# The first norm's sum of squares: sixteen ones products on TensorE behind the projection's blocks, in place of sixteen VectorE additions

## What is computed

```python
def rmsnorm(x, g):
    xf = x.astype(F32)
    y = xf * lax.rsqrt(jnp.mean(xf * xf, axis=-1, keepdims=True) + RMS_EPS)
    return (y * g.astype(F32)).astype(x.dtype)

def s5_layer(h, g_pre, ...):
    xn = rmsnorm(h, g_pre)
    uz = xn @ w_in                 # 2048 x 4096
    u, z = jnp.split(uz, 2, axis=-1)
    y = s5_ssm(u, ...)             # needs powers of the state's poles, made from its parameters
    ...
```

## Time and profile before

| | |
|---|---|
| median of 3 runs | 3483.96 us |
| the three runs | 3482.14, 3483.96, 3485.89 us |
| profiled execution, device time | 3486.52 us |
| its span in the profile | 3484.7 us |
| PE busy | 3246.0 us (93%) |
| PEld busy | 2529.4 us (73%) |
| DVE busy | 1435.7 us (41%) |
| ACT busy | 1145.8 us (33%) |
| POOL busy | 1619.3 us (46%) |

### The profile page before, as it was taken

How to read it: one execution, slowest core, us unless ns; L and a number is a source line. 1 busy time by engine, 2 the same in 40 slices (tenths; PEclk the granted TensorE clock), 3 DMA queues, 4 the chain that set the end, 5 groups by cost and what they waited for, 6 DMA issues and landing times.

```text
span 3484.7 us, 48561 instructions
## 1 busy us (share of the span) xinstructions
PE 3246.0 (93%) x18540; PEld 2529.4 (73%) x18540; DVE 1435.7 (41%) x2229; ACT 1145.8 (33%) x1500; POOL 1619.3 (46%) x1292
## 2 busy tenths in 40 slices
PE   5799998999899999999989889999999999967797
PEld 4688886878668787878868757777777777734486
DVE  8777783120242222222230144444534534546512
ACT  4344442233333332322342333323223323315521
POOL 2566662444557667777744424344444434400142
PEclk9899998999999999999999999999999999978899
DMA  3555555232212222222212222222212212211222
GB/s 129 156 155 161 160 164 156 96 143 88 95 57 80 81 84 84 84 84 84 82 61 99 84 103 82 82 74 85 81 71 73 89 68 83 79 57 48 92 92 94
DMA packets 117903, 332.97 MB, mean 96 GB/s; under 512 B 58512, under 2 KB 61712, under 8 KB 86544
## 3 DMA queue, kind: packets, MB, share of 16 engines
q1 hardware_dynamic: 117776, 331.08, 28.2%
HBM read 296.96 MB, written 29.36 MB: 94 GB/s over the span
## 4 chain that ended last, share of the span: by engine, by line
PE 73%; issue 16%; POOL 5%; DVE 4%; ACT 1%; DMA 0%; ACTq 0%; SPq 0%; POOLq 0%; DVEq 0%
PE bank L159 21%; PE bank L161 20%; PE bank L160 20%; POOL wlo L146 4%; PE bank L1308 2%; PE bank L1014 1%; PE bank L1032 1%; PE bank L422 1%; ACT whi L140 1%; PE bank L421 1%; PE bank L433 1%; PE bank L407 1%; PE bank L1023 0%; PE bank L999 0%; PE bank L1288 0%
## 5 line engine op out<-in xcount | busy, mean ns | idle before, releaser
L146 POOL TENSOR_TENSOR wlo<-wraw,whi 128x512 fp32r<-128x512 f32 x912 | 1245.3, 1397 | 1685.9 <-ACT whi L140 1685.8
L159 PE MATMUL bank<-rhi,whi 128*128 128x512 f32 x3648 | 1494.2, 410 | 108.3 <-POOL wlo L146 37.5
L160 PE MATMUL bank<-rlo,whi 128*128 128x512 f32 x3648 | 1433.8, 393 | 0.0
L161 PE MATMUL bank<-rhi,wlo 128*128 128x512 f32 x3648 | 1433.7, 393 | 0.0
L159 PEld LDWEIGHTS bank<-rhi,whi 128*128 128x128 f32 x3648 | 691.8, 190 | 326.2 <-issue 92.7
L161 PEld LDWEIGHTS bank<-rhi,wlo 128*128 128x128 f32 x3648 | 691.8, 190 | 148.9
L160 PEld LDWEIGHTS bank<-rlo,whi 128*128 128x128 f32 x3648 | 693.3, 190 | 140.9 <-issue 11.3
L140 ACT ACTIVATE whi<-wraw 128x2048 fp32r<-128x2048 f32 x228 | 437.0, 1917 | 617.9 <-PE bank L161 471.0
L845 POOL TENSOR_TENSOR wraw<-wraw,vec 128x512 f32<-128x512 f32 x260 | 266.3, 1056 | 0.0
L753 DVE TENSOR_TENSOR ssum<-ssum,wk 128x512 f32<-128x512 f32 x30 | 21.6, 719 | 311.4 <-ACT wk L743 311.4
L743 ACT ACTIVATE wk<-bank 128x512 f32<-128x512 f32 x32 | 27.8, 870 | 236.7 <-PE bank L161 236.7
(11 more groups left out here) (351 smaller groups left out, 3252.5 us busy)
## 6 DMA issues: line engine op xcount, KB each, us to landing
wraw<-in_wall_dram SPq DMA_DIRECT2D x228, 1024.0 KB, 4.8
g<-in_bmat_dram SPq DMA_DIRECT2D x16, 512.0 KB, 5.4
g<-scr_e SPq DMA_DIRECT2D x128, 64.0 KB, 4.8
scr_a<-ssum SPq DMA_DIRECT2D x32, 256.0 KB, 2.1
g<-in_xp_dram SPq DMA_DIRECT2D x4, 1024.0 KB, 11.7
g<-in_cmat_dram SPq DMA_DIRECT2D x16, 256.0 KB, 4.5
scr_u<-wk SPq DMA_DIRECT2D x16, 256.0 KB, 5.9
scr_y<-wk SPq DMA_DIRECT2D x16, 256.0 KB, 2.2
```

The source lines that it names most:

```text
L146: ins = pool.tensor_tensor(wlo[:, slot, c], wraw[:, slot, c], whi[:, slot, c].bitcast(F32), ALU.subtract)
L159: pe.matmul(acc[slot][:, :], whk, rhi[:, k, :], start=(k == 0), stop=False)
L160: pe.matmul(acc[slot][:, :], whk, rlo[:, k, :], start=False, stop=False)
L161: ins = pe.matmul(acc[slot][:, :], wlk, rhi[:, k, :], start=False, stop=(k == KT - 1))
```

## The change

The square of each block is no longer added by DVE. PE multiplies it by the ones matrix right behind the block's three products, accumulating over the 16 blocks in the norm's PSUM bank, and PE's ones product increments `ssq`, which gives ACT its square buffer back. The final ones product over `ssum` goes. The square root waits for `ssq` at 16 in place of `st_mm`; the later waits on `st_mm` count one less.

```diff
-        def split_lo(d, src, gain, base, square=None, ks=range(KT)):
+        def split_lo(d, src, gain, base, ks=range(KT)):
...
-                if square is not None:
-                    add_square(d, *square, k)
-
-        def add_square(d, sqb, sbase, k):
-
-            d.wait_ge(sq_f, sbase + k + 1)
-            wait(d, ssq, sbase + k)
-            if isinstance(k, int) and k == 0:
-                d.tensor_copy(ssum[:, :], sqb[0]).then_inc(ssq, 1)
-            else:
-                d.tensor_tensor(ssum[:, :], ssum[:, :], sqb[k % 2], ALU.add).then_inc(ssq, 1)
...
-        def project_summing(pe, n, slot, r_base, sq_base):
+        def project_summing(pe, n, slot, r_base, sq_base, sqb):
...
-            norm_root(act, V_EPS6, st_mm, 1)
+            norm_root(act, V_EPS6, ssq, 16)
...
-            split_lo(d, g1, V_G1, 0, (sqb0, 0))
+            split_lo(d, g1, V_G1, 0)
...
-            project(pe, 0, 0, wait_r=0)
-            norm_sum(pe, 0)
+            project_summing(pe, 0, 0, 0, 0, sqb0)
...
-            project_summing(pe, N_GATE, 0, 48, 16)
+            project_summing(pe, N_GATE, 0, 48, 16, sqb)
```

More of the change, by code:

```diff
@@ L1856, in _ @@
                 act_out(act, n, n % 2, n // 2, n - 48, V_GPOST0, 16, True, scaled=(n - 62) or None)
-            norm_root(act, V_EPS6, st_mm, 2)
+            norm_root(act, V_EPS6, st_mm, 1)
             act.wait_ge(gemm, N_GATE)
@@ L1877, in _ @@
             act_out(act, N_LORA - 1, 0, (N_LORA - 1) // 2, 15, V_GPOST1, 48, False)
-            norm_root(act, V_EPS6, st_mm, 3)
+            norm_root(act, V_EPS6, st_mm, 2)
             act.wait_ge(gemm, N_LORA)
@@ L1911, in _ @@
             act_last(act, 227, 1, 113, 15, more=False)
-            norm_root(act, V_EPS5, st_mm, 4)
+            norm_root(act, V_EPS5, st_mm, 3)
         @block.vector
@@ L2016, in _ @@
             norm_sum(pe, 3)
-            project_summing(pe, N_LORA, 1, 80, 32)
+            project_summing(pe, N_LORA, 1, 80, 32, sqb)
             for n in range(N_LORA + 1, N_RWKV + 4):
```

## The result

| | median | runs |
|---|---|---|
| before | 3485.81 us | 20 (3481.14 to 3494.22) |
| changed | 3493.11 us | 20 (3487.58 to 3500.11) |
| ratio | 1.0017 | 95% interval 1.0010 to 1.0024 |

By the ratio the change costs 5.9 us (3.5 to 8.4), by the medians 7.3 us. A second set, 12 runs of the changed kernel beside 29 of before, gave a ratio of 1.0019 (1.0009 to 1.0029). The kernel is slower: both intervals leave out 1. The profiled execution took 3492.37 us (span 3490.6), the one of before 3486.52 (span 3484.7). On the page of the profile DVE's busy time fell from 1435.7 to 1428.4 us and PE's rose from 3246.0 to 3256.5.

The account below looks back on a forecast made before the run. DVE bounded the first norm's stage at 1.27 us a block; PE at 1.56 takes over. Block 15's square, root and reciprocal come 7.8 us later, undiminished to the end: 3483.96 + 7.8 = 3491.8 us, 8-in-10 range 3486 to 3495.5.

Parts of the forecast that it names:

- What bounds: First norm's stage: DVE sets the rhythm at 1.27 us a block, ACT is next at 1.13 us.
- PE's block: First norm's stage, changed: three products 0.69 us plus ones product 0.87 us, so 1.56 us a block at full rate.
- The ring of square buffers: ACT's square of block k waits for ones product k-2; 1 us of room, so PE runs unstalled.
- The ramp: PE's start at 26.19 us: half rate for 5.0 us, each microsecond of it costing 0.48 us.
- The tail on ACT: End of the norm: square of block 15 at 50.67 us, `whi`, table load, root at 54.4, 0.6 us after PE.
- No drain beside the table load: ACT's table load before the root: no drain in the rows; the page's 1.38 us would make the sum 9.2 us.
- Rigid path: From reciprocal past the handover at 153.57 us to the end: the 7.8 us delay passes through undiminished.
- a sign against it: Whole kernel: the forecast would be wrong if the end moved by another amount than the handover.
- The number: Whole kernel: 7.8 us slower, median 3491.8 us, 0.22% more; 63 in 100 for slower by over 7.0 us.
- The cheap ones product: Rival, norm stage: ones product under 0.43 us, ACT sets the rhythm, 3482 us, no measurable change; 4 in 100.
- Half rate throughout: Rival, norm stage: PE stays at half rate, 2.99 us a block, some 28 us more, 3512 us; 4 in 100.
- Absorption: Rival, DVE's part behind the norm: hidden slack leaves 0 to 4 us, 3484 to 3488 us; 9 in 100.

Follow-up runs that it names:

- e_both: Kernel before, DVE's additions kept, with an unused ones product on x behind each block of tile 0; one run 3490.92 us beside 3487.42.
- e_warm: Changed kernel with seven unused ones products on PE ahead of block 0; 3491.30 us beside 3487.42, ratio 1.0009.
- e_root_first: Changed kernel with ACT's root ahead of `whi` of tile 1; one run 3492.80 us.
- e_f32r_early: Changed kernel with one-pass ones products, three square buffers, early parameter operations and first power step ahead of the reciprocal; 3480.52 us beside 3485.74, ratio 0.9980.
- e_double: Changed kernel with each of the first norm's sixteen ones products done twice; 3508.06 us beside 3487.42 for before, ratio 1.0054.
- e_early: Changed kernel with DVE's first 15 parameter operations moved between the blocks' rests and ACT's sines moved earlier; 3486.62 us beside 3485.74, ratio 0.9999.
- e_f32r: Changed kernel with squares and ones in the 32-bit type PE takes in one pass; 3485.48 us beside 3487.42, ratio 0.9996.
- e_before_early: Kernel before, DVE's additions kept, with 15 parameter operations moved early between the blocks' rests; 3486.50 us beside 3486.65, ratio 1.0001.
- e_f32r_early2: Changed kernel with one-pass ones products, three square buffers and early parameter operations, first power step left behind `z_scale`; 3477.38 us beside 3486.65, ratio 0.9971.
- changed again: The changed kernel itself, unaltered, measured once more against before; 3492.81 us beside 3485.74, ratio 1.0019.

## Why the prediction was right

**What bounds.** DVE held the stage at 1.27 us a block and PE had too little room; the additions' removal is in the timeline as 0.81 us of idle DVE time. Right.

**PE's block.** 1.56 us forecast, 1.55 us measured, and two records in every block, unstalled. The price came from the two places where line 786 stood already. This term carried the forecast; doubling it doubled the delay and a one-pass product removed it.

**The ring of square buffers.** ACT waits in it 0.30 us a block, but PE never waits for a square: right, and `e_both`, with ones products and without that wait, shows the same delay.

**The ramp.** 5.0 us assumed, 4.3 us in the profiled execution: the record at 29.88 in the changed kernel (0.55 us) is the first shortened one. Starting at full rate gave 1.97 us back, which is 0.46 us for each of the 4.3, beside 0.48 in the sum.

**The tail on ACT.** Root directly behind the table load: right. The square of block 15 came at 49.96 us instead of 50.67 and the reciprocal at 54.43 instead of 55.1. Of these 0.7 us PE's earlier start explains 0.3 and the shorter ramp another 0.3. Counted from PE's start the reciprocal is 7.3 us later; the sum said 7.8.

**No drain beside the table load.** In the changed kernel the root follows the start of its load by 53.71 - 52.41 = 1.30 us, and this time nothing else could have hidden a drain: PE's last ones product had ended at 53.03. Ahead of the next load there is none either: the root ends at 54.40 and the load starts at 54.41. The estimate of 9.2 us from the Trainium skill ("ScalarE: Activation LUTs", "What ACT_TABLE_LOAD costs") is refuted for this place; the measurement decides.

**Rigid path.** 7.04 us at the reciprocal, 7.49 at the handover, 5.85 at the last reciprocal. No delay was absorbed up to the handover: right. The 0.45 us that it grew come just ahead of the handover, most of them where DVE's line 352 idles 0.69 us for PE's line 433 instead of 0.26. So DVE does wait for PE there, which the prediction's "and not the other way" passed over. Behind the handover the end moved by another amount than the handover did, and the prediction had named that as a sign against it. The 1.6 us lost there were no slack, but PE's rate. In before PE was at half rate from 154.1 to 164.0 us, 9.9 us. In the changed kernel it was at full rate until some 163.3 and at half rate until 169.9, 6.6 us. The 3.3 us less, at 0.48 each, are the 1.6 us. PE's timeline of the changed kernel, stretch 160 to 178:

```profile
161.78 0.39 PE L422 MATMUL bank<-wk,g 128*128 128x63 f32 x2
```

PE's timeline of before, stretch 153 to 172, at the same point of its work:

```profile
154.51 0.63 PE L422 MATMUL bank<-wk,g 128*128 128x63 f32 x2
```

The granted clock agrees; the first row is a stretch of before, the second one of the changed kernel, and the clock is the third number from the end, 0.50 in both:

```profile
154.10:164.00 9.90, 9.90 (x39) 9.04 (x38) 7.62 (x10) 0.60 (x1) 0.00 (x0) 0.50 0.23 56
163.30:169.90 6.60, 6.60 (x24) 5.73 (x24) 5.96 (x8) 0.60 (x1) 0.00 (x0) 0.50 0.29 72
```

In both kernels PE had idled 1.9 us just ahead of the handover. From handover to first loop the executions show one of two lengths, 14.0 us (before, `e_warm`, `e_root_first`, `e_f32r_early`, `e_double`) or 12.4 us (changed in both its profiled executions, `e_both`, `e_early`, `e_f32r`, `e_before_early`, `e_f32r_early2`), not ordered by what was changed. Which of them an execution gets is open, and so is whether the changed kernel gets the short one more often. The forecast had left PE's rate behind the handover out of its bounds; it should have stood there with 1.6 us.

**The number.** Forecast 7.8 us, measured 5.9 (3.5 to 8.4) by the ratio and 7.3 by medians. Direction and size hold, the forecast within the interval. The text gave 63 in 100 to more than 7.0 us, with its middle only 0.8 us beyond. By the ratio it came out below, by the medians above, and the interval takes in both: on which side it fell is luck. By the marks the handover moved 7.5 us, near the forecast; it is the 1.6 us behind it that bring the end of the profiled execution down to 5.85.

**Which rivals are out.** The cheap ones product: 0.87 us here too. Half rate throughout: products 0.23 us apart from 30.2 us on. Absorption: refuted by the doubled products, 13.2 of 13.6 us at the handover.

## What to carry to other kernels

Before work is moved to an engine that looks idle in a stage, compare rhythms: the block time of the engine that would be relieved, and that of the engine that takes the work, with the addition priced at the same shape and type. Here 1.27 us fell to ACT's 1.13 on one side and rose to 1.56 on the other, and a type whose ones product takes 0.23 us instead of 0.87 took the second away. Relief of an engine is worth something only when its idle time is filled, and what is moved into it must be checked against its new neighbours: here four short operations beside POOL's `wlo` cost 3.8 us, more than the 3.3 us of the step that was moved, and in `e_before_early` the same neighbour cost 4.0.

## What was not expected

**Where the scatter comes from.** Executions of one kernel differ by up to 13 us, those of before too. The marks place most of it behind the third norm. From that norm's reciprocal to the last one the profiled executions took 1470.1 to 1470.3 us (five kernels), 1472.8 to 1473.0 us (before, the changed kernel twice, `e_warm`) or 1478.0 to 1479.8 us (`e_double`, `e_early`, `e_f32r_early`), with the same instructions. The difference grows in a stretch some 1100 to 1300 us behind the mark, where PE is busy about 70% of the time. The stretch rows are for before and then for `e_early`; the columns are PE, PEld, DVE, ACT and POOL busy with their counts, granted clock, DMA share and GB/s.

```profile
3094.30:3194.30 100.00, 67.95 (x236) 39.50 (x236) 61.58 (x145) 44.45 (x112) 0.00 (x0) 0.75 0.18 66
3194.30:3294.30 100.00, 72.95 (x283) 44.45 (x283) 64.50 (x151) 54.57 (x129) 0.00 (x0) 0.85 0.15 58
```

```profile
3095.10:3195.10 100.00, 68.59 (x224) 38.70 (x225) 60.86 (x144) 42.57 (x107) 0.00 (x0) 0.72 0.19 64
3195.10:3295.10 100.00, 72.90 (x266) 41.96 (x265) 58.53 (x142) 49.72 (x126) 0.00 (x0) 0.81 0.09 29
```

The granted clock is 0.75 and 0.85 in the one and 0.72 and 0.81 in the other, and PE gets through 519 and 490 matmul records in the same 200 us. The same two stretches of other executions go along: 0.78 and 0.85 in `e_f32r` (1470.1 us), 0.75 and 0.85 in the changed kernel (1472.9), 0.72 and 0.81 in `e_f32r_early` (1479.8). That the clock's moments of change within this stage set the time is what these rows suggest, not what they show; why they fall as they do in a given execution stays open, and it was not tried to steer them. For a change of a few us near the start, the marks of one profiled execution say more than its time.

**The ramp varies.** From nearly the same start, PE stayed at half rate (1.2 GHz, products 0.43 us apart) for 4.3, 4.6, 5.0 and 6.1 us (changed, changed again, before, `e_early`), as placed by the first shortened record of each. In a stage that PE bounds this alone is worth 0.9 us. The profile's granted clock doesn't show this ramp. It stands at 1.00 in the changed kernel from 25.9 to 30.2 us, where the products are 0.43 us apart, though behind the handover it read 0.50 for the same spacing:

```profile
25.90:30.20 4.30, 4.30 (x8) 2.79 (x9) 1.18 (x2) 0.94 (x2) 0.00 (x0) 1.00 0.00 0
```

At the start of the kernel PE's rate is therefore read from the starts of its records.

**Two operations beside POOL.** Short DVE operations that lie wholly beside POOL's subtraction take 1.17 to 1.42 us in these traces, whatever their own length of 0.23 to 0.36 us, about the length of one of POOL's four instructions (1.24 us). An addition of 128x512 takes 1.77 us instead of 0.69. Not every operation is lengthened: the reciprocal beside the same work stays at 3.35 us, and a copy of 128x64 at 0.20.
